# Chunk scan of a recurrent mixer: triangular levels as 32x32 blocks, and a head transpose four steps later

## The reference

```
def step(state, inp):
    r_t, w_t, k_t, v_t, a_t, b_t = inp
    sa = jnp.einsum('bhvk,bhk->bhv', state, a_t)
    state = (state * w_t[:, :, None, :]
             + sa[..., None] * b_t[:, :, None, :]
             + v_t[..., None] * k_t[:, :, None, :])
    return state, jnp.einsum('bhvk,bhk->bhv', state, r_t)
```

```
proj = h @ w_in
qa, ka, va, za, q_idx, k_idx, w_idx, qb, kb, vb, zb = jnp.split(proj, COL_SPLITS, axis=-1)
qa = _rms_norm(qa.reshape(heads_a), q_norm_a)
```

## Time and profile before

| what | us |
|---|---|
| median of 3 runs | 1937.65 (1937.49 to 1940.42) |
| profiled execution | 1941.16 |
| its span in the trace | 1939.4 |
| PE matmul busy | 1866.6 (96%) |
| POOL busy | 1360.6 (70%) |
| DVE busy | 1090.6 (56%) |
| ACT busy | 808.2 (42%) |
| the scan, first to last | 963.87 to 1081.05 |

### The profile page before, as it was taken

One profiled execution on the slowest core, in us unless ns is written; L12 is line 12 of the kernel. 1 busy time (PEld: TensorE's weight loads), 2 busy tenths in 40 slices (PEclk: granted clock), 3 DMA queues, 4 the chain that ended last, 5 costly groups with the idle time before them and its releaser, 6 DMA issues.

```text
span 1939.4 us, 31618 instructions
## 1 busy us (share of the span) xinstructions
PE 1866.6 (96%) x12631; PEld 1552.6 (80%) x12631; DVE 1090.6 (56%) x1163; ACT 808.2 (42%) x1088; POOL 1360.6 (70%) x683
## 2 busy tenths in 40 slices
PE   5999999999999999999899899999999999999997
PEld 1678778888668898888699678888888888888886
DVE  1115747551243546878654564778888888923223
ACT  3334444444454554344322544433333334333333
POOL 2657777888339889965334598999999988844442
PEclk8999999999999999999999999999999999999999
DMA  9994455555785565543100345555555555555553
GB/s 361 372 326 161 153 173 174 190 180 195 252 290 174 172 191 192 178 144 133 48 4 4 105 160 193 194 179 188 186 182 191 179 192 179 179 191 191 193 193 130
DMA packets 174430, 352.55 MB, mean 182 GB/s; under 512 B 6735, under 2 KB 19421, under 8 KB 171773
## 3 DMA queue, kind: packets, MB, share of 16 engines
q1 hardware_dynamic: 173084, 346.84, 53.9%
q10 hardware_dynamic: 1249, 4.31, 0.6%
HBM read 349.02 MB, written 2.10 MB: 181 GB/s over the span
## 4 chain that ended last, share of the span: by engine, by line
PE 63%; POOL 14%; issue 10%; DVE 8%; DMA 3%; ACT 2%; SPq 1%; POOLq 0%; DVEq 0%; ACTq 0%
PE bank L931 20%; POOL WL L573 13%; PE bank L933 10%; PE bank L885 8%; PE bank L887 8%; PE bank L886 8%; PE bank L1363 5%; DMA arena<-in_w_ada 3%; PE bank L954 1%; DVE CV L2499 1%; SPq L633 1%; PE bank L1281 1%; DVE CV L2504 1%; DVE half L2362 1%; PE bank L1326 1%
## 5 line engine op out<-in xcount | busy, mean ns | idle before, releaser
L573 POOL TENSOR_TENSOR WL<-WR,WH 128x1024 fp32r<-128x1024 f32 (+2 forms) x516 | 1264.2, 2472 | 421.6 <-ACT WH L1587 420.3
L1587 ACT ACTIVATE WH<-WR 128x1024 fp32r<-128x1024 f32 (+2 forms) x560 | 576.1, 1036 | 773.7 <-PE bank L887 432.3
L931 PE MATMUL bank<-HX,WH 128*128 128x512 f32 x1840 | 650.9, 399 | 1.0 <-POOL WL L573 1.0
L933 PE MATMUL bank<-HX,WL 128*128 128x256 f32 x1840 | 516.5, 281 | 0.0
L931 PEld LDWEIGHTS bank<-HX,WH 128*128 128x128 f32 x1840 | 345.7, 188 | 87.5 <-POOL WL L573 1.9
L885 PE MATMUL bank<-WH,HX 128*128 128x512 f32 (+2 forms) x864 | 341.2, 395 | 6.7 <-POOL WL L573 6.6
L933 PEld LDWEIGHTS bank<-HX,WL 128*128 128x128 f32 x1840 | 347.5, 189 | 0.1
L887 PE MATMUL bank<-WH,HX 128*128 128x512 f32 (+2 forms) x864 | 332.1, 384 | 0.0
L886 PE MATMUL bank<-WL,HX 128*128 128x512 f32 (+2 forms) x864 | 331.7, 384 | 0.0
L885 PEld LDWEIGHTS bank<-WH,HX 128*128 128x128 f32 x864 | 163.1, 189 | 48.7 <-issue 15.4
L887 PEld LDWEIGHTS bank<-WH,HX 128*128 128x128 f32 x864 | 163.0, 189 | 31.2
(11 more groups left out here) (319 smaller groups left out, 2052.9 us busy)
## 6 DMA issues: line engine op xcount, KB each, us to landing
WR<-in_w_in SPq DMA_DIRECT2D x96, 1024.0 KB, 5.0
WR<-in_ffn_w_gate SPq DMA_DIRECT2D x44, 1024.0 KB, 5.1
WR<-in_ffn_w_up SPq DMA_DIRECT2D x44, 1024.0 KB, 5.2
WR<-in_ffn_w_down SPq DMA_DIRECT2D x44, 1024.0 KB, 5.1
arena<-in_w_ada SPq DMA_DIRECT2D x64, 512.0 KB, 10.4
WR<-in_w_out SPq DMA_DIRECT2D x32, 1024.0 KB, 5.1
WR<-in_w_ada SPq DMA_DIRECT2D x16, 1024.0 KB, 5.1
WR<-in_w_in SPq DMA_DIRECT2D x12, 768.0 KB, 4.4
```

The source lines that it names most:

```text
L573: eng.tensor_tensor(half(WL, n % NSLOT, *w), half(WR, n % NSLOT, *w), half(WH, nth(n) % 2, *w), ALU.subtract).then_inc(ready, 1)
L931: pe.matmul(bank[:, :].rearrange("p (h n) -> p h n", h=2), wh[:, k, o], hx[:, :, kk, :], start=kk == 0, stop=False, skip_group_check=True)
L933: last = pe.matmul(bank[:, 0:L], wl[:, k, o], hx[:, 0, kk, :], start=False, stop=kk == KT - 1, skip_group_check=True)
L1587: act.activation(half(WH, nth(n) % 2, *w), half(WR, n % NSLOT, *w), ACT.Copy).then_inc(hi_ready, 1)
```

## The change

`B` is 32. The levels keep only the two diagonal 32x32 blocks of each 64x64 matrix: `Xi`, `T2`, `LM` and the new `Zc` hold 32 columns per head pair. `blocks` makes one product of a set as 16 matmuls of 32x32, each on the diagonal tile of its own 32 partitions. The last level combines the two blocks: its T takes the off-diagonal block straight from the masked LB, on tiles from rows 0 to 31 (64 to 95) to columns 32 to 63 (96 to 127), 8 matmuls, and its Z goes back the same way; both are only copied by DVE. `Zi` is put together at the end: its left half at level 4, its right half at level 5. The triangular product L is made by `block_products`, the diagonal blocks alone, and a second time transposed (LT), ahead of LB; DVE copies LT, and POOL makes its masks from that copy with six instructions per set instead of seven, over 128 instead of 256 elements. The second head turn stands at step 10 of its chunk instead of step 6. Ahead of the scan POOL folds the masks once more to 32 columns and makes one mask less.

```diff
-        Xi, T2, P1, Us = ([at(16384 + 512 * i + 256 * s_, 4, N) for s_ in range(2)] for i in range(4))
-        LM = [[at(18432 + 1280 * s_ + 256 * i, 4, N) for i in range(5)] for s_ in range(2)]
+        B = N // 2
+        Xi, T2 = ([at(16384 + 512 * i + 256 * s_, 4, B) for s_ in range(2)] for i in range(2))
+        P1, Us = ([at(17408 + 512 * i + 256 * s_, 4, N) for s_ in range(2)] for i in range(2))
+        LM = [[at(18432 + 1280 * s_ + 256 * i, 4, B) for i in range(4)] for s_ in range(2)]
+        LT, Zc = ([at(19456 + 1280 * s_ + 128 * i, 4, B) for s_ in range(2)] for i in range(2))
         ST = [at(20992 + 256 * s_, 4, N) for s_ in range(2)]
-        level = [masks[:, N * i:N * (i + 1)] for i in range(6)]
+        level = [masks[:, B * i:B * (i + 1)] for i in range(5)]
...
-        pe_names = both("LB", "L") + both("AK") + both("BK") + both("V") + levels_pe
+        pe_names = both("L", "LB") + both("AK") + both("BK") + both("V") + levels_pe
         act_names = both("BK") + both("V") + levels_act
-        dve_names = both("LB", "L", "X0") + both("AK") + levels_dve
-        pool_names = both("M1", "Zm", "Z0", "M2", "M3", "M4", "M5")
+        dve_names = both("LT", "L", "X0", "LB") + both("AK") + levels_dve
+        pool_names = both("M1", "Zm", "Z0", "M2", "M3", "M4")
...
-                L_.mark(pool.tensor_tensor(LM[s][m - 1], LBr[c % 2][s][:, :, 1, :],
-                                           level[m].unsqueeze(1).to_broadcast([P, 4, N]), ALU.mult), f"M{m}_{s}")
+                L_.mark(pool.tensor_tensor(LM[s][m - 1], LT[s], level[m].unsqueeze(1).to_broadcast([P, 4, B]), ALU.mult),
+                        f"M{m}_{s}")
 
             for c in range(NCH):
                 for s in range(2):
-                    D_.wait(pool, f"LB_{s}", c)
+                    D_.wait(pool, f"LT_{s}", c)
                     below_level(1, s, c)
-                    if c >= 2:
-                        S_.wait(pool, f"U_{s}", c - 2)
-                    z = Zi[c % 2][s]
-                    L_.mark(pool.tensor_tensor(z, LBr[c % 2][s][:, :, 1, :], level[0].unsqueeze(1).to_broadcast([P, 4, N]),
-                                               ALU.mult), f"Zm_{s}")
+                    if c >= 1:
+                        P_.wait(pool, f"Z{LEVELS - 1}_{s}", c - 1)
+                    z = Zc[s]
+                    L_.mark(pool.tensor_tensor(z, LT[s], level[0].unsqueeze(1).to_broadcast([P, 4, B]), ALU.mult), f"Zm_{s}")
                     L_.wait(pool, f"Zm_{s}", c)
-                    L_.mark(pool.tensor_tensor(z, z, I2.unsqueeze(1).to_broadcast([P, 4, N]), ALU.add), f"Z0_{s}")
-                    for m in range(2, LEVELS):
+                    L_.mark(pool.tensor_tensor(z, z, I1.unsqueeze(1).to_broadcast([P, 4, B]), ALU.add), f"Z0_{s}")
+                    for m in range(2, LEVELS - 1):
...
-                    if kk == 6:
+                    if kk == (6, 10)[c]:
...
+            block_rows = [slice(B * i, B * i + B) for i in range(4)]
+            first_rows, second_rows = block_rows[0::2], block_rows[1::2]
+
+            def blocks(s, bank, stat, mov, out_rows=block_rows, in_rows=block_rows):
+
+                o = BANK[4 * s + bank][:, 0:4 * B].rearrange("p (q n) -> p q n", q=4)
+                for q in range(4):
+                    for to, at_rows in zip(out_rows, in_rows):
+                        last = pe.matmul(o[to, q, :], stat[at_rows, q, :], mov[at_rows, q, :], start=True, stop=True)
+                return last
...
+            def block_products(s, c0, x, y):
+
+                o = BANK[4 * s + 3][:, c0:c0 + 4 * B].rearrange("p (q n) -> p q n", q=4)
+                for q in range(4):
+                    for i in range(2):
+                        for hi, h in enumerate(halves):
+                            n = slice(B * i, B * i + B)
+                            last = pe.matmul(o[block_rows[2 * hi + i], q, :], x[h, 4 * s + q, n], y[h, 4 * s + q, n],
+                                             start=True, stop=True)
+                return last
...
+                    block_products(s, 4 * B, b_, a_)
+                    P_.mark(block_products(s, 0, a_, b_), f"L_{s}")
                     P_.mark(four(s, 0, 0, 2 * C, (of_set(b_, s), of_set_ra(c, s))), f"LB_{s}")
-                    P_.mark(four(s, 3, 0, C, (of_set(a_, s), of_set(b_, s))), f"L_{s}")
...
-                        L_.wait(pe, f"M{m}_{s}", c)
+                        if m < LEVELS - 1:
+                            L_.wait(pe, f"M{m}_{s}", c)
                         if m == 1:
                             D_.wait(pe, f"X0_{s}", c)
                         else:
                             A_.wait(pe, f"X{m - 1}_{s}", c)
                         if m == 4 and c >= 1:
                             DS_.wait(pe, f"Sum_{s}", c - 1)
-                        P_.mark(four(s, 3, 0, N, (of_pair(LM[s][m - 1]), of_pair(Xi[s]))), f"T{m}_{s}")
+                        if m < LEVELS - 1:
+                            P_.mark(blocks(s, 3, LM[s][m - 1], Xi[s]), f"T{m}_{s}")
+                        else:
+                            D_.wait(pe, f"LB_{s}", c)
+                            P_.mark(blocks(s, 3, LBr[par][s][:, :, 1, B:N], Xi[s], second_rows, first_rows), f"T{m}_{s}")
...
-                            P_.mark(four(s, 0, 0, N, (of_pair(Zi[par][s]), of_pair(T2[s]))), f"X{m}_{s}")
-                        P_.mark(four(s, 1, 0, N, (of_pair(T2[s]), of_pair(Zi[par][s]))), f"Z{m}_{s}")
+                            P_.mark(blocks(s, 0, Zc[s], T2[s]), f"X{m}_{s}")
+                            P_.mark(blocks(s, 1, T2[s], Zc[s]), f"Z{m}_{s}")
+                        else:
+                            P_.mark(blocks(s, 1, T2[s], Zc[s], first_rows, second_rows), f"Z{m}_{s}")
...
+                    P_.wait(dve, f"L_{s}", c)
+                    D_.mark(dve.tensor_copy(LT[s], bankq(s, 3, 4 * B)), f"LT_{s}")
+                    D_.mark(dve.tensor_tensor(T2[s], bankq(s, 3), fourb(level0), ALU.mult), f"L_{s}")
+                    D_.wait(dve, f"L_{s}", c)
+                    D_.mark(dve.tensor_tensor(Xi[s], T2[s], fourb(I1), ALU.add), f"X0_{s}")
                     P_.wait(dve, f"LB_{s}", c)
                     D_.mark(dve.tensor_tensor(LBr[par][s], heads4x2(BANK[4 * s][:, :]), blocks, ALU.mult), f"LB_{s}")
-                    P_.wait(dve, f"L_{s}", c)
-                    D_.mark(dve.tensor_tensor(T2[s], bank4(s, 3), four(level0), ALU.mult), f"L_{s}")
-                    D_.wait(dve, f"L_{s}", c)
-                    D_.mark(dve.tensor_tensor(Xi[s], T2[s], four(I2), ALU.add), f"X0_{s}")
...
-                        D_.mark(dve.tensor_tensor(T2[s], bank4(s, 3), four(I2), ALU.add), f"T{m}_{s}")
+                        D_.mark(dve.tensor_tensor(T2[s], bankq(s, 3), fourb(I1), ALU.add) if m < LEVELS - 1 else
+                                dve.tensor_copy(T2[s], bankq(s, 3)), f"T{m}_{s}")
                     for s in range(2):
                         P_.wait(dve, f"Z{m}_{s}", c)
-                        D_.mark(dve.tensor_copy(Zi[par][s], bank4(s, 1)), f"Z{m}_{s}")
+                        if m == LEVELS - 2:
+                            dve.tensor_copy(Zc[s], bankq(s, 1))
+                            ins = dve.tensor_scalar(Zi[par][s][:, :, 0:B], bankq(s, 1), first_block, None, ALU.mult)
+                        else:
+                            ins = dve.tensor_copy(Zc[s] if m < LEVELS - 1 else Zi[par][s][:, :, B:N], bankq(s, 1))
+                        D_.mark(ins, f"Z{m}_{s}")
```

More of the change, by code:

```diff
@@ L305, in build @@
         upto_diag, below = low_block[:, 0, :], low_block[:, 1, :]
-        level0 = masks[:, 960:1024]
+        level0, I1 = masks[:, 960:992], masks[:, 992:1024]
         I2 = masks[:, 1024:1088]
@@ L811, in level_mask @@
                                             pattern=[[2 * b, nb], [0, b]], channel_multiplier=-1))
-                fold(dst, block_tmp)
+                fold(fold_tmp, block_tmp)
+                fold_block(dst, fold_tmp)
             level_mask(level0, 1, 0)
-            for m in range(LEVELS):
+            for m in range(LEVELS - 1):
                 level_mask(level[m], 1 << m, 1)
```

10 lines of the change are left out of this document (9 added, 1 removed).

## The result

The change made the kernel slower: 1981.15 us median of 4 runs (1978.55 to 1982.82) against 1937.57 us of the kernel before in the same session (1932.46 to 1940.42). The ratio is 1.0235, 95% interval 1.022 to 1.025, which is +43.6 us where 21.5 us less were predicted. The profiled execution of after took 1978.55 us, its span is 1976.8 us.

The account below looks back on a forecast made before the run. The scan was taken as bound by PE's pace, the second head turn by DVE's scaling. Scan -15.2 and turn -6.2 us gave 1937.65 - 21.5 = 1916 us, 8-in-10 range 1909 to 1930.

Parts of the forecast that it names:

- Pace of small matmuls: Chunk scan: 32 ns for a round of four records, so a 16-matmul product falls from 0.467 to 0.254 us.
- Rival 1: Scan: pace is per matmul, one per 58 ns, not per tile; scan 178.6 us, kernel 1994, slower; chance 0.06.
- Rival 3: Scan: clock falls to 0.50 for 3.4 to 5.1 us stretches; kernel 1923 to 1926, up to 1936; chance 0.11.
- Rival 2: Scan: 58 ns is a floor per pass; scan 122.3 us, kernel 1937; chance 0.08 for rounds of 45 to 60 ns.
- Changes of shape: Scan: each switch of PE tile shape costs 0.13 us, 40 in all, 5.2 us; bounds 0 to 8.
- Evictions: Scan levels: 128x128 copies take 0.295 us on DVE, 0.277 on ACT; POOL's masks at most 0.746.
- The level of 1.89 us: Scan, chunk 0: with PE shorter and evictions in view, a level lasts 1.89 us instead of 3.08.
- The head turn: Token chunks near 213 us: turning four steps later removes PE's wait and low clock, -6.2 us (-4 to -6.7).
- The sum: Whole kernel: scan -15.2 us and head turn -6.2 us, 1937.65 - 21.5 = 1916 us against the median.

Follow-up runs that it names:

- loop (f): Kernel before plus 640 discarded f32 32x32 matmuls ahead of the scan, in a hardware loop of 64: 13.9 us for them in all.
- micro: Kernel before plus discarded PE matmuls ahead of the scan, looped and written out: 640 of 32x32 took 33.7 us written out, 13.9 in a loop of 64.
- pairs: Kernel after, levels 1 to 4 with one matmul for two head pairs, 768 fewer in the scan, results not the reference's: 1931.04 us, ratio 0.9971 to before.
- loop0: Kernel after, chunk 0's levels 1 to 4 as a hardware loop, waits on extra matmuls, level 1's masks throughout: 1973.06 us; same written out 1980.93.
- loop (e): Kernel before plus a discarded loop ahead of the scan, 16 matmuls of 32x32 and 8 of 64x64 in turn, 20 times: 0.995 us a turn.
- turn10: Kernel before with only the second head turn moved, from step 6 to step 10 of its chunk: 1931.21 us, ratio 0.9974.
- loop (c): Kernel before plus 320 discarded 64x64 matmuls ahead of the scan, in a hardware loop of 8: 0.467 us per 8 at full clock.

## Why the prediction was wrong

**The step that failed** is in "Pace of small matmuls": "I therefore take 32 ns for a round of four records: 16 matmuls (32 records) are 8 rounds, 0.254 us". As a property of the array it was nearly right: 34 ns a round in loop (f), 0.27 us a product. But in the kernel a product of 16 takes 16 x 58 = 0.93 us where it comes in a stalled stretch, because the instructions for it come at 3.73 us per 64 matmuls. The working asked what the array and the four engines could do and never what brings PE its instructions. The rows that would have asked it were in the trace of before: 28 instruction packets of 16,384 bytes in the scan, some only 3.5 to 3.8 us apart, against 15 to 34 us in nearly all of the dense stretches before it. Nothing showed that they couldn't come faster, since the 64x64 records need a block per 3.73 us. But with 2688 matmuls in place of 1728 they had to come every 2.35 us (101.2 us for 43 blocks), a pace of which no stretch of the trace gave an example.

**Rival 1** (0.06) is what happened, with another mechanism. It said "PE is dealt its matmuls at the pace of rows 3, one per 58 ns" and gave 178.6 us for the scan and 1994 for the kernel; it was 163.65 and 1981. I read it as too high because a block can be brought while PE waits or works on the 64x64 products, which the layout with a fixed cost per matmul doesn't give back. Its turning point, 30 ns per matmul, was passed by a factor of nearly two. What I held against it, four matmuls started within 0.03 us, is a burst out of instructions that were there; it says nothing of a stretch of thousands. The sentence for it, "nowhere in the trace does a long stretch run faster", deserved the weight.

The Trainium skill (Runtime: NRT & Kernel Launch, Instruction fetch mechanics) says that each sequencer fills its instruction memory in 16 KiB blocks over a DMA queue of its own, and calls the cost "mostly hidden". The block size and the queue agree with the packets here; that it is hidden does not hold for small matmuls, with 31.4 us of stalls of PE on line 1386 alone. It gives 128 KiB for PE's memory; here a loop of 64 KB stayed and one of 128 KB didn't, and nothing between was run.

**Rival 3**, the clock, came too, far beyond its 3.4 to 5.1 us a chunk: 0.74 to 0.78 granted over the whole scan. As a cause it fell: blocks last 3.8 us at either level in after, in micro the small matmuls written out stall and looped don't, and the clock is back in pairs. Where it can cost is in the dense 64-row products that follow the stalls, which I haven't separated; an estimate is the 3 us by which the scan exceeds 43 x 3.73 us. The two overlap, though: PE's idle time for "issue" in the scan is 35.6 us (31.4, 2.2 and 2.0 on lines 1386, 1396 and 1375), and the scan is 62 us longer than the 101.2 forecast. The other 27 us are not separated; loop0 suggests that most of them are the low clock, which would come into view if the instructions came faster.

**Rival 2**, a floor per pass, is out: 34 ns a round in the loop.

**Changes of shape**: 0.13 us forecast, 0.13 measured in loop (e), with a loop's edge in one of the two. In the kernel they aren't separated; most can fall into the stalls.

**Evictions**: 0.295, 0.277 forecast; 0.292 and 0.277 measured, POOL's masks 0.455, well under the bound of 0.746. The level of 1.89 us never came about, as PE's instructions were late next, not the evictions.

**The head turn**: -6.2 us forecast, -5.0 (-3.1 to -7.0) measured alone. The idle time went and the clock stayed up; the wait that comes back at the next turn is 1.4 us, not up to 0.5.

**The sum**: -5.0 for the turn, +46.3 for the scan (163.65 - 117.38), +1.7 behind it (from one profiled execution of each, unexplained): +43.0, against +43.6 measured.

turn10 is the one version here that still computes the recurrence and beats both kernels, by 0.3%: 0.9974 of before.

## What to carry to other kernels

Splitting matmuls into smaller ones pays only while PE's instructions keep up: in written-out code count the instructions (four per f32 matmul, two in bf16), and compare 3.7 us per 256 of them with the array's time for the same stretch. Where the array would be faster, use fewer and larger matmuls, or a hardware loop of up to 64 KB (with its edge and its waits priced: the levels looped here were no faster than the old ones), and look in the trace for bursts of 128 weight loads with "issue" between them. When a pace is read from a profile, ask how many independent limits could lie just at it: here two lay within some per cent of each other.

## What the runs showed of the hardware

- PE's instructions arrive as packets of 16,384 bytes on a queue of their own. In written-out code a block lasts 3.7 us on average (3.35 to 4.04) however short the bursts are, though its packet itself takes only 0.9 to 1.5 us. The rest lies between a packet's landing and the first load out of it (1.2 to 1.6 us) and between that load and the next packet (1.0 to 1.7 us in micro); what PE's sequencer does in these two stretches stays open.
- Small tiles are as quick as their size says: 8.4 ns between loads of 32x32 on four tiles over 512 loads in a row. The Trainium skill (TensorE: Matmul & The Clock Gate, Back-to-back issue gap) puts about 25 ns on each matmul of up to 64 columns as an issue floor; here two passes each on four tiles took 16.8 ns per matmul.
- A hardware loop's edge costs PE 0.33 us between the last load of a turn and the first of the next, with bodies of 16 to 64 KB of 32x32 matmuls; in loop (c), eight 64x64 matmuls in 0.467 us, none shows.
- A wait that has long been satisfied costs PE 68 ns between 64x64 matmuls when it is an instruction of its own, more than the matmul's own 58 ns.
